# Row-block projections widened to 512 columns, and the order of work around each norm's transposes changed, in a two-block transformer forward pass

## Chip, cores and metric

One core of one Trainium2 chip. The metric is the device time of one execution in microseconds (us), as the median of repeated executions.

## The reference

256 tokens of width 1024 go through two blocks, all in float32. The first has an "even" layer (differential attention, a gated short convolution, cross attention to a 256-token memory) and an "odd" layer (forgetting attention, cross attention), each behind an RMS norm. The second has HGRN2 with a convolution, then a pooling mixer, each followed by cross attention and a gated feed-forward, with a layer norm behind every one of the six steps:

```python
for l in range(DEPTH):                       # DEPTH = 2
    y = hybrid_ab_mixer(x, ...) if l == 0 else multiscale_pool_mixer(x, ...)
    x = layer_norm(ALPHA * x + y, ln_mix_g[l], ln_mix_b[l])
    y = memory_cross_attention_2(x, mem_n, xa_wq[l], xa_wk[l], xa_wv[l], xa_wo[l])
    x = layer_norm(ALPHA * x + y, ln_xa_g[l], ln_xa_b[l])
    y = swiglu_ffn(x, ffn_wg[l], ffn_wu[l], ffn_wd[l])        # D_FF = 2816
    x = layer_norm(ALPHA * x + y, ln_ffn_g[l], ln_ffn_b[l])
```

## The kernel before

**Weights come in units of 1 MB**, 194 of them, in the order of the list PHASES. A unit is loaded by SyncE (SP) into one of two slots of w_raw; ScalarE (ACT) rounds each half of it to w_hi (`hi`, line 1119) and VectorE (DVE) puts the remainder into w_lo (`lo`, line 1675); TensorE (PE) then forms each float32 product as three fp32r products, hi·hi, hi·lo, lo·hi (`passes`, lines 502 to 504). SP loads unit v once the remainder of unit v-2 is made; ACT rounds a half of unit v once PE is done with that half of unit v-2. All engines run fixed programs and meet at semaphores: lo_done and half_done count two per unit, evacuated counts evictions.

**Three kinds of unit.** A K8 unit (`k8_unit`) is 1024 rows by 256 columns of a matrix and takes 48 products 256 columns wide. With weights_stationary the weights are loaded into the array and the tokens move; the result is transposed. Without it the tokens are loaded, 128 at a time, and the 256 weight columns move: these are the row blocks. Each K8 unit fills one PSUM bank; banks 0 and 1 take turns, so that a bank is evicted by ACT (`step`, `copy_out`, line 1141) while the next unit runs. A DN unit (`down_unit`) is 256 rows by 1024 columns, 24 products 512 wide into four banks that stay open over the phase. A feed-forward unit (`half_unit`, lines 836 and 838) loads weights and moves u_hi and u_lo together (512 wide) and u_hi alone (256 wide): 32 products.

**Turns.** A normed activation must be transposed before the next projection. There are nine turns: mem, x, h1 (RMS), h2 (the plain residual), mem2, mix0, xa0, mix1, xa1. PE transposes (`turn_pairs` line 599, `turn_tile` line 610) four groups into banks 6 and 7, ACT rounds each to u_hi (`turned_hi`, `tile_hi` line 1197), DVE writes u_lo (`turned_lo`, `tile_lo` line 1797) and raises tL. A transpose of group n waits for tL of group n-2. In layer norms the last DN unit signals its first token tile by tile0_out and the second by half_done; DVE adds the residual (`res_tile`, line 1816), takes statistics (`tile_ask`, line 1699; the power is POOL's) and norms (`norm_tile`, lines 1737 and 1740). Two K8 units that don't need the new activation run on PE meanwhile (`kv_beside_turn`, `beside_norm`; xk1a, xk1b, half of xv1, o_kv); h2 and xa1 have none.

**The order around a turn before.** ACT, in the second of those units: `hi` of half 0 of the unit after next, first tile, eviction, second tile, `hi` of half 1. DVE (`norm_beside`, `split_beside`): residual and statistics of tile 0, residual of tile 1, a `lo`, statistics of tile 1, norm of tile 0, a `lo`, norm of tile 1, then tile 0's remainder, `lo`, tile 1's remainder, `lo`. At h2 DVE norms the second block's memory (four operations, lines 1737 and 1740) ahead of the residual.

## Time and profile before

| | |
|---|---|
| median of 3 executions | 1379.06 us (1378.71 to 1382.15) |
| the profiled execution's own time | 1384.16 us |
| its span in the trace | 1382.4 us |
| PE / DVE / ACT busy | 94% / 65% / 49% |
| mean granted clock of PE | 0.97 of full |
| chain that ended last | PE 77%, DVE 12%, ACT 4%, DMA 3%, issue 3% |
| bytes read from HBM | 217.54 MB, 158 GB/s |

Busy time of PE counts from the start of a product to its modelled end, and products overlap in it; how long a product holds the engine is read from one start to the next. In timelines the columns are start, length, engine and line, operation, tiles, shapes, count, and in brackets the idle time before it and what ended it. A granted clock of 1.00 is 2.4 GHz, 0.50 is 1.2 GHz.

### The profile page before, as it was taken

Reading aid. Unit: us, or ns where it says so; the run is one execution under the profiler, and the core shown is the slowest. Engines: PE = TensorE matmul, PEld = TensorE weight load, DVE = VectorE, ACT = ScalarE, POOL = GpSimd, SP = SyncE. Lnnn points to the kernel's source line nnn. Section 1 sums busy time; section 2 is a strip of 40 time slices with the busy share of each in tenths; the row PEclk is TensorE's granted clock in tenths of the full one; section 3 lists DMA queues with packets and bytes.
Section 4 is the critical chain, followed back from the end, with each engine's and each line's share of the span. In section 5 each row is a group of like instructions: output and inputs, shape, how many; then the busy total and the mean of one; then the engine's idle time right before and its main releaser. Section 6 shows DMA issues by size and latency. Waiting matters only on the chain.

```text
span 1382.4 us, 21858 instructions
## 1 busy us (share of the span) xinstructions
PE 1304.6 (94%) x8566; PEld 1189.4 (86%) x8566; DVE 898.5 (65%) x1281; ACT 682.1 (49%) x1082; POOL 63.3 (5%) x72
## 2 busy tenths in 40 slices
PE   6999998999999998989989899899999998899996
PEld 6999997889999997889988798788888896788885
DVE  6566576775756555579977755666667755666666
ACT  5445676454436777347424353444444353444442
POOL 0012001000110000000000000000000100000000
PEclk9999999999989999999999999899999999899998
DMA  7455533254535332644425543665555443455552
GB/s 241 158 186 183 174 124 123 96 180 153 188 119 158 114 123 92 230 144 152 153 92 164 171 153 122 227 201 189 182 182 183 137 169 122 150 185 183 184 187 84
DMA packets 167923, 219.67 MB, mean 159 GB/s; under 512 B 3691, under 2 KB 151478, under 8 KB 167846
## 3 DMA queue, kind: packets, MB, share of 16 engines
q1 hardware_dynamic: 164502, 206.68, 45.6%
q0 software_dynamic: 3040, 11.20, 2.6%
q8 instruction: 53, 0.87, 0.3%
q10 hardware_dynamic: 304, 0.73, 0.1%
q14 instruction: 24, 0.20, 0.0%
HBM read 217.54 MB, written 1.05 MB: 158 GB/s over the span
## 4 chain that ended last, share of the span: by engine, by line
PE 77%; DVE 12%; ACT 4%; DMA 3%; issue 3%; POOL 1%; DVEq 0%; SPq 0%; ACTq 0%
PE bank L502 16%; PE bank L504 16%; PE bank L503 16%; PE bank L836 12%; PE bank L838 6%; DVE w_lo L1675 3%; DVE small L1699 1%; DVE h L1816 1%; ACT w_hi L1119 1%; PE bank L713 1%; PE bank L742 1%; DVE att L1737 1%; PE bank L729 1%; DVE att L2273 1%; DMA w_raw<-in_o_w_out 1%
## 5 line engine op out<-in xcount | busy, mean ns | idle before, releaser
L1675 DVE TENSOR_TENSOR w_lo<-w_raw,w_hi 128x1024 fp32r<-128x1024 f32 x388 | 472.2, 1224 | 303.4 <-ACT w_hi L1119 298.2
L1119 ACT ACTIVATE w_hi<-w_raw 128x1024 fp32r<-128x1024 f32 x388 | 408.9, 1058 | 433.1 <-PE bank L504 247.8
L836 PE MATMUL bank<-u_s,w_hi 128*128 128x512 f32 x704 | 254.5, 405 | 1.1 <-DVE u_s L1797 1.1
L502 PE MATMUL bank<-w_hi,y_hi 128*128 128x512 f32 (+1 forms) x656 | 234.4, 357 | 4.5 <-DVE w_lo L1675 3.5
L503 PE MATMUL bank<-w_lo,y_hi 128*128 128x512 f32 (+1 forms) x656 | 229.5, 350 | 0.0
L504 PE MATMUL bank<-w_hi,y_lo 128*128 128x512 f32 (+1 forms) x656 | 229.5, 350 | 0.0
L838 PE MATMUL bank<-u_s,w_lo 128*128 128x256 f32 x704 | 199.9, 284 | 0.0
L502 PE MATMUL bank<-w_hi,u_s 128*128 128x256 f32 x672 | 193.1, 287 | 2.2 <-DVE w_lo L1675 2.2
L503 PE MATMUL bank<-w_lo,u_s 128*128 128x256 f32 x672 | 191.2, 285 | 0.0
L504 PE MATMUL bank<-w_hi,u_s 128*128 128x256 f32 x672 | 191.2, 284 | 0.0
L836 PEld LDWEIGHTS bank<-u_s,w_hi 128*128 128x128 f32 x704 | 134.9, 192 | 35.5 <-DVE u_s L1797 1.9
L502 PE MATMUL bank<-u_s,w_hi 128*128 128x256 f32 x544 | 157.8, 290 | 2.1 <-DVE u_s L1797 2.1
L503 PE MATMUL bank<-u_s,w_hi 128*128 128x256 f32 x544 | 155.3, 285 | 0.0
L504 PE MATMUL bank<-u_s,w_lo 128*128 128x256 f32 x544 | 155.3, 285 | 0.0
L502 PEld LDWEIGHTS bank<-w_hi,y_hi 128*128 128x128 f32 x656 | 125.5, 191 | 23.1 <-DVE w_lo L1675 2.8
L504 PEld LDWEIGHTS bank<-w_hi,y_lo 128*128 128x128 f32 x656 | 125.3, 191 | 16.6
L503 PEld LDWEIGHTS bank<-w_lo,y_hi 128*128 128x128 f32 x656 | 125.6, 191 | 15.0
L838 PEld LDWEIGHTS bank<-u_s,w_lo 128*128 128x128 f32 x704 | 135.5, 192 | 0.7
L502 PEld LDWEIGHTS bank<-w_hi,u_s 128*128 128x128 f32 x672 | 130.1, 194 | 3.0 <-DVE w_lo L1675 2.6
L503 PEld LDWEIGHTS bank<-w_lo,u_s 128*128 128x128 f32 x672 | 130.1, 194 | 0.0
L504 PEld LDWEIGHTS bank<-w_hi,u_s 128*128 128x128 f32 x672 | 130.0, 194 | 0.0
L502 PEld LDWEIGHTS bank<-u_s,w_hi 128*128 128x128 f32 x544 | 105.9, 195 | 3.2 <-DVE u_s L1797 3.2
(296 smaller groups left out, 1642.4 us busy)
## 6 DMA issues: line engine op xcount, KB each, us to landing
w_raw<-in_e_w_in SPq DMA_DIRECT2D x28, 1024.0 KB, 5.1
w_raw<-in_o_w_in SPq DMA_DIRECT2D x28, 1024.0 KB, 5.2
w_raw<-in_ffn_wg SPq DMA_DIRECT2D x22, 1024.0 KB, 5.3
w_raw<-in_ffn_wu SPq DMA_DIRECT2D x22, 1024.0 KB, 5.4
w_raw<-in_ffn_wd SPq DMA_DIRECT2D x22, 1024.0 KB, 5.0
w_raw<-in_ab_w_in SPq DMA_DIRECT2D x12, 1024.0 KB, 5.1
w_raw<-in_e_w_out SPq DMA_DIRECT2D x8, 1024.0 KB, 4.9
w_raw<-in_o_w_out SPq DMA_DIRECT2D x8, 1024.0 KB, 5.0
```

Of the source, the lines that this page charges most:

```text
L502: pe.matmul(out_ap, ah, bh, start=start, stop=False, skip_group_check=True)
L503: pe.matmul(out_ap, ah, bl, start=False, stop=False, skip_group_check=True)
L504: return pe.matmul(out_ap, al, bh, start=False, stop=stop_, skip_group_check=True)
L713: mm = pe.matmul(bank[SC[pr]][:, SEQ * m:SEQ * m + SEQ], XQT[:, 2 * hd + j, P * m:P * m + P], (KT2 if g < 32 else KT1)[:, 2 * hd + j, :], ...
L729: mm = pe.transpose(bank[PTB][:, dst:dst + P], s[:, src:src + P], ident)
L742: mm = pe.matmul(o[:, SEQ * j:SEQ * j + SEQ], V2[:, k, cs], p[:, SEQ * k:SEQ * k + SEQ], start=(k == 0), stop=(k == 1))
L836: pe.matmul(two(bank[banks[m]][:, :], SEQ), w_hi[:, a:a + P], u_both[:, :, SEQ * k:SEQ * k + SEQ], start=(k == 0), stop=False, skip_group_ ...
L838: mm = pe.matmul(bank[banks[m]][:, 0:SEQ], w_lo[:, a:a + P], uh[:, k, :], start=False, stop=(k == 7), skip_group_check=True)
L1119: act.activation(w_hi[:, at:at + 1024], w_raw[:, at:at + 1024], ACT.Copy).then_inc(hi_done, 1)
L1675: v.tensor_tensor(w_lo[:, at:at + 1024], w_raw[:, at:at + 1024], w_hi[:, at:at + 1024].bitcast(F32), ALU.subtract).then_inc(lo_done, 1)
L1699: mark(v.bn_stats(bn6[:, 12 * m + 6 * j:12 * m + 6 * j + 6], src[:, m, 512 * j:512 * j + 512]))
L1737: mark(v.scalar_tensor_tensor(nrm[:, m], src[:, m], mv[:, m, 0:1], gain, ALU.subtract, ALU.mult))
```

## The change

Row blocks: two adjacent units now hold rows 0 to 511 and rows 512 to 1023 of the same 512 columns (`pairs` on SP). PE makes 24 products 512 wide of each into two banks, one per token tile, that stay open over the pair (`row_unit`). ACT evicts both at the pair's end, bank 0 on row0_done, bank 1 on half_done (`row_step`). 58 units are paired: e_kv 4, e_nat 14, e_beside 4, o_kv 4, o_nat 20 of 28, ab_nat 4, xv0 4, xv1 4. In the odd layer the value units now come two by two, with two gate units between. Keys of that layer are normed as 8 and 4 heads, before 6 and 6.

Turns: transposes use four banks, 6, 7, 2, 3, and wait for tL of group n-4. ACT serves both tiles ahead of `hi` (`turn_step`). DVE takes each bank's residual and statistics when that bank is signalled (bank_out). `split_beside` makes the next unit's `lo` first and both remainders after it. At h2 the memory norm comes behind the turn. In the RMS turns the remainders go ahead of one `lo`. At xa1 the first gate and up units run token tile by token tile (`gate_up_tiles`): tile 0 of both, with tile 1's transpose between, then tile 1 of both.

```diff
+            def row_unit(slot, part, banks, xh, xl, wait_lo, wait_bank, fresh=None, between=None):
+                for half in range(2):
...
+                    pe.wait_ge(lo_done, wait_lo + half)
+                    for m in range(2):
+                        if part == 0 and half == 0 and wait_bank is not None:
+                            pe.wait_ge(evacuated, wait_bank + m)
+                        for j in range(2):
+                            k = 4 * part + 2 * half + j
+                            at = 2048 * slot + 1024 * half + 512 * j
+                            mm = passes(bank[banks[m]][:, :], ((xh[:, k, P * m:P * m + P], xl[:, k, P * m:P * m + P]),
+                                                               (w_hi[:, at:at + 512], w_lo[:, at:at + 512])),
+                                        k == 0, k == 7)
+                        if part == 1 and half == 1 and m == 0:
+                            mm.then_inc(row0_done, 1)
+                    mm.then_inc(half_done, 1)
...
-                        if m == 0:
-                            mm.then_inc(tile0_out, 1)
+                            if m == 0 or n == 0:
+                                mm.then_inc(bank_out, 1)
...
-                    pe.wait_ge(tL, n - 1)
+                    pe.wait_ge(tL, n - 3)
...
-                        mm = pe.transpose(bank[6 + n % 2][:, P * k:P * k + P], src[:, m, c:c + P], ident)
+                        mm = pe.transpose(bank[TURN_BANKS[n % 4]][:, P * k:P * k + P], src[:, m, c:c + P], ident)
...
+                def half_tile(slot, banks, half, tile, signal):
+                    ts = slice(P * tile, P * tile + P)
+                    for m in range(2):
+                        o = two(bank[banks[m]][:, :], SEQ)
+                        for k in range(4 * half, 4 * half + 4):
+                            a = 2048 * slot + SEQ * k + P * m
+                            pe.matmul(o[:, :, ts], w_hi[:, a:a + P], u_both[:, :, SEQ * k + P * tile:SEQ * k + P * tile + P],
+                                      start=(k == 0 and tile == 0), stop=False, skip_group_check=True)
+                            mm = pe.matmul(o[:, 0, ts], w_lo[:, a:a + P], uh[:, k, ts],
+                                           start=False, stop=(k == 7 and tile == 1), skip_group_check=True)
...
+            def turn_step(u, first, evac, second):
+                v = u + 2
+                first()
+                evac()
+                second()
+                for half in range(2):
+                    hi(v % 2, half, 16 * (v // 2 + 1), 2 * u + 1 + half)
...
+            def row_step(u, part, pair, banks, out_, i=None, between=None, after=None):
...
+                hi(v % 2, 0, i_land + 16 * (v // 2 + 1), i_half + (2 * u + 1))
...
+                if part == 1:
+                    act.wait_ge(row0_done, pair + 1 if i is None else i + (pair + 1))
+                    out_(0, banks[0])
+                act.wait_ge(half_done, i_half + (2 * u + 2))
+                if part == 1:
+                    out_(1, banks[1])
...
+                hi(v % 2, 1, i_land + 16 * (v // 2 + 1), i_half + (2 * u + 2))
...
             def norm_beside(out_name, name):
 
                 last = UNIT0[out_name] + COUNT[out_name] - 1
-                res_tile(out_name, 0, ALPHA)
-                tile_ask(hv, name, 0)
-                res_tile(out_name, 1, ALPHA)
+                for m in range(2):
+                    for n in range(2):
+                        res_stats(out_name, m, n, ALPHA)
+                    stats_ask(name, m)
                 lo_of(last + 2, 0)
-                tile_ask(hv, name, 1)
                 layer_norm_tile(name, 0)
                 lo_of(last + 2, 1)
                 layer_norm_tile(name, 1)
 
             def split_beside(first):
 
-                tile_lo(uh, ul, 0)
-                lo_of(first, 0)
-                tile_lo(uh, ul, 1)
-                lo_of(first, 1)
+                for half in range(2):
+                    lo_of(first, half)
+                for m in range(2):
+                    tile_lo(uh, ul, m)
                 for half in range(2):
                     lo_of(first + 1, half)
...
+            turned_lo(uh, ul, GCOL["o_norm_g"], 4)
             lo_of(kv + 3, 0)
-            turned_lo(uh, ul, GCOL["o_norm_g"], 4)
             lo_of(kv + 3, 1)
...
-            v.wait_ge(mem_ln_in, 32)
-            for m in range(2):
-                norm_tile(nrm, "mem2", m, MLG, MLB).then_inc(nrm_ready, 1)
             stream("o_out", 6, 1)
...
             stream("o_out", 7, 1)
+            v.wait_ge(mem_ln_in, 32)
+            for m in range(2):
+                norm_tile(nrm, "mem2", m, MLG, MLB).then_inc(nrm_ready, 1)
             stream("ab_t", 0, 1)
...
+                    up1 = UNIT0["ffn1"] + 1
+                    for n in range(2):
+                        res_stats("xo1", 0, n, ALPHA)
+                    stats_ask("xa1", 0)
+                    res_stats("xo1", 1, 0, ALPHA)
+                    layer_norm_tile("xa1", 0)
+                    res_stats("xo1", 1, 1, ALPHA)
+                    stats_ask("xa1", 1)
+                    tile_lo(uh, ul, 0)
+                    layer_norm_tile("xa1", 1)
+                    lo_of(up1, 0)
+                    tile_lo(uh, ul, 1)
+                    lo_of(up1, 1)
```

## Rows read from the trace of the kernel before

**Rows 1.** The page, its part 1: TensorE's busy time.
```profile
PE 1304.6 (94%) x8566; PEld 1189.4 (86%) x8566; DVE 898.5 (65%) x1281; ACT 682.1 (49%) x1082; POOL 63.3 (5%) x72
```

**Rows 2.** Waits of PE, waiter and releaser: us in total, times, longest.
```profile
PE bank L610 <- DVE u_s L1797: 11.6, 4, 5.2
...
PE bank L610 <- DVE h L1740: 6.5, 1, 6.5
...
PE bank L599 <- DVE u_s L1785: 5.7, 2, 3.7
```

**Rows 3.** Groups by shape, PE: first product of each row-block triple on normed rows.
```profile
L502 PE MATMUL bank<-w_hi,u_s 128*128 128x256 f32 x672 | 193.1, 287 | 2.2 <-DVE w_lo L1675 2.2
```

**Rows 4.** Timeline of PE (start, length): first and last L502, 256 wide, then 512 wide.
```profile
74.07 0.28 PE L502 MATMUL bank<-w_hi,u_s 128*128 128x256 f32 x1
...
80.55 0.28 PE L502 MATMUL bank<-w_hi,u_s 128*128 128x256 f32 x1
...
261.27 0.58 PE L502 MATMUL bank<-w_hi,y_hi 128*128 128x512 f32 x1
...
293.47 0.39 PE L502 MATMUL bank<-w_hi,y_hi 128*128 128x512 f32 x1
```

**Rows 5.** Timeline of PE, two of the 48 products 12 columns wide, 23 apart.
```profile
380.12 0.25 PE L504 MATMUL bank<-cf_hi,u_s 128*128 128x12 f32 x1
...
382.69 0.25 PE L503 MATMUL bank<-cf_lo,u_s 128*128 128x12 f32 x1
```

**Rows 6.** Timeline of DVE, ACT and PE at the turn mix0.
```profile
786.41 1.28 DVE L1740 SCALAR_TENSOR_TENSOR h<-att,pow_out,nat 128x1024 f32<-128x1024 f32 x1
792.04 1.29 DVE L1797 TENSOR_TENSOR u_s<-bank,u_s 128x512 fp32r<-128x512 f32 x2 [4.34 <-ACT u_s L1197]
...
790.47 1.06 ACT L1119 ACTIVATE w_hi<-w_raw 128x1024 fp32r<-128x1024 f32 x1 [6.60 <-DMA w_raw<-in_xa_wq]
...
795.38 0.58 PE L502 MATMUL bank<-u_s,w_hi 128*128 128x256 f32 x1 [0.56 <-DVE u_s L1797]
```

**Rows 7.** The same at the turn xa0.
```profile
868.79 1.28 DVE L1740 SCALAR_TENSOR_TENSOR h<-att,pow_out,nat 128x1024 f32<-128x1024 f32 x1
...
874.07 1.06 ACT L1119 ACTIVATE w_hi<-w_raw 128x1024 fp32r<-128x1024 f32 x1 [7.82 <-DMA w_raw<-in_ffn_wu]
...
878.98 0.80 PE L836 MATMUL bank<-u_s,w_hi 128*128 128x512 f32 x1 [0.56 <-DVE u_s L1797]
```

**Rows 8.** The same at the turn h2 (588.11: last of four of its kind).
```profile
588.11 1.28 DVE L1740 SCALAR_TENSOR_TENSOR att<-att,pow_out,nat 128x1024 f32<-128x1024 f32 x1
...
592.97 1.09 PE L610 MATMUL bank<-cst,h 128*128 128x128 f32 x8 [2.78 <-DVEq L2238]
...
597.78 0.58 PE L502 MATMUL bank<-u_s,w_hi 128*128 128x256 f32 x1 [0.56 <-DVE u_s L1797]
```

**Rows 9.** Timeline of PE: first product behind the turns xa1 and mix1.
```profile
1182.49 0.80 PE L836 MATMUL bank<-u_s,w_hi 128*128 128x512 f32 x1 [0.56 <-DVE u_s L1797]
...
1108.49 0.39 PE L502 MATMUL bank<-u_s,w_hi 128*128 128x256 f32 x1 [1.03 <-DVE u_s L1797]
```

**Rows 10.** Windows: length, PE, PEld, DVE, ACT, POOL busy (count); granted clock; DMA share; GB/s.
```profile
597.80:601.30 3.50, 3.50 (x16) 3.50 (x17) 2.96 (x3) 0.05 (x1) 0.00 (x0) 0.50 0.00 0
795.40:799.30 3.90, 3.90 (x18) 3.90 (x19) 3.81 (x4) 1.00 (x2) 0.00 (x0) 0.50 0.14 43
879.00:884.60 5.60, 5.60 (x17) 4.82 (x18) 4.09 (x4) 1.00 (x2) 0.00 (x0) 0.50 0.89 300
...
893.00:904.10 11.10, 11.10 (x64) 9.61 (x63) 6.70 (x11) 5.67 (x10) 0.00 (x0) 1.00 0.58 196
```

**Rows 11.** Timeline of DVE: the last layer norm begins.
```profile
1374.19 1.28 DVE L1737 SCALAR_TENSOR_TENSOR att<-h,small,nat 128x1024 f32<-128x1024 f32 x1 [0.24 <-DVE pow_in L1730]
```

**Rows 12.** Timeline of ACT: a late weight copy, and the eviction behind it.
```profile
374.11 1.06 ACT L1119 ACTIVATE w_hi<-w_raw 128x1024 fp32r<-128x1024 f32 x1 [3.79 <-DMA w_raw<-in_o_w_in]
375.07 0.58 ACT L1141 ACTIVATE nat<-bank 128x512 f32 x1
```

More of the change, by code:

```diff
@@ L60, with pair_of @@
 COUNT = {name: n for name, _, n in PHASES}
+PAIRS = (("e_kv", 2), ("e_nat", 7), ("e_beside", 2), ("o_kv", 2), ("o_nat", 10), ("ab_nat", 2), ("xv0", 2), ("xv1", 2))
+PAIR0 = {}
+_k = 0
+for _name, _n in PAIRS:
+    PAIR0[_name] = _k
+    _k += _n
+def pair_of(name, j):
+    if name == "o_nat" and j >= 14:
+        return None if j >= 26 or (j - 14) % 4 >= 2 else PAIR0[name] + 7 + (j - 14) // 4
+    if name not in PAIR0 or j >= 2 * dict(PAIRS)[name]:
+        return None
+    return PAIR0[name] + j // 2
 def unit_end(name):
@@ L117, in z_unit @@
     name, before, _, _ = BESIDE["o"]
-    first = {"C": 1, "Y": C_HEADS}[kind]
-    return BANK0[name] + before + first + (2 if kind == "C" else 1) * (hd // 2) + 1
+    z = hd // 2
+    return BANK0[name] + before + (4 * (z // 2) + 2 + z % 2 if kind == "C" else C_HEADS + z) + 1
 G1_ROWS = [("e_mem_norm_g", 8), ("e_norm_g", 8)]
@@ L393, in k8, with pairs, unit @@
                 return base + n
+            def pairs(base, w, c0, n):
+                def unit(base_j, half, i):
+                    rows_of = w[512 * half:512 * half + 512, :]
+                    src = rows_of[:, bass.ds(512 * i + c0, 512)] if i is not None else rows_of[:, c0:c0 + 512]
+                    v = 2 * base_j - 2
+                    load(base_j % 2, base_j < 2, v if i is None else 4 * i + v, src.rearrange("(k p) n -> p k n", p=P))
+                if n < 4:
+                    for half in range(2):
+                        unit(base + half, half, None)
+                else:
+                    with sp.Fori(0, n // 2) as i:
+                        for half in range(2):
+                            unit(base + half, half, i)
+                return base + n
             def dn(base, w, n, order=None):
@@ L519, in k8_unit @@
                         for k in range(4 * half, 4 * half + 4):
-                            at = 2048 * slot + SEQ * k
-                            o = bank[bk][:, SEQ * m:SEQ * m + SEQ]
-                            first = half == 0 and m == 0 and k == 0
-                            end = k == 7
-                            if weights_stationary:
-                                a = at + P * m
-                                mm = passes(o, ((w_hi[:, a:a + P], w_lo[:, a:a + P]), (xh[:, k, :], xl[:, k, :])),
-                                            first, end)
-                            else:
-                                mm = passes(o, ((xh[:, k, P * m:P * m + P], xl[:, k, P * m:P * m + P]),
-                                                (w_hi[:, at:at + SEQ], w_lo[:, at:at + SEQ])), first, end)
@@ L531, in k8_unit @@
-                    mm.then_inc(half_done, 1)
-            def k8_phase(name, xh, xl, weights_stationary, n=None, skip=0, fresh=None):
+                            a = 2048 * slot + SEQ * k + P * m
+                            mm = passes(bank[bk][:, SEQ * m:SEQ * m + SEQ],
+                                        ((w_hi[:, a:a + P], w_lo[:, a:a + P]), (xh[:, k, :], xl[:, k, :])),
+                                        half == 0 and m == 0 and k == 0, k == 7)
+                    mm.then_inc(half_done, 1)
@@ L657, in st_turn_qk @@
                     pe.wait_ge(qk_ready, {"A": 1, "X": 2, "C": 3, "Y": 5}[kind])
-                if kind == "C" and hd == C_HEADS // 2:
+                if kind == "C" and hd == 8:
                     pe.wait_ge(qk_ready, 4)
@@ new lines, in row_stream @@
+            def row_stream(name, skip, n, dst, func=ACT.Copy):
+                base, kb = UNIT0[name] + skip, BANK0[name] + skip
+                if n >= 4:
+                    with act.Fori(0, n // 2) as i:
+                        for j in range(2):
+                            row_step(base + j, j, pair_of(name, skip), (kb % 2, (kb + 1) % 2), row_out(dst, i, func), i)
+                else:
+                    for j in range(n):
+                        row_of(name, skip + j, row_out(dst, 0, func))
@@ L1323, in attention @@
                         continue
+                    if kind == "K8" and pair_of(phase, j) is not None:
+                        row_of(phase, j, row_out(eV, j // 2) if name == "e" else row_out(oV, (j - before) // 4),
+                               between=exponentials)
+                        continue
                     if kind == "DN":
@@ L1570, in _ @@
                 if layer == 1:
-                    stream("xv1", 0, 2, nat_dst(V2))
+                    row_stream("xv1", 0, 2, V2)
                     for c in range(4):
```

322 lines of the change are left out of this document (192 added, 130 removed).

## Prediction

> **What bounds the kernel now.** The page comes first: PE is busy 94% of the span, DVE 65% [rows 1]. The table of waits shows what PE's idle time is: its largest entries are transposes (lines 599 and 610) that wait for DVE around a turn [rows 2]. So the streams between the turns go at PE's pace, and a turn costs what its chain takes. The group of the row blocks gives their number [rows 3]: 672 triples, 42 units of 16; with 16 units on the memory they are the 58 that the change pairs. The pace is read from starts in the timeline [rows 4]: from 74.07 to 80.55 us there are 54 products 256 wide, 0.120 us each; from 261.27 to 293.47 there are 141 products 512 wide, 0.228 us each. Last I read the two queues around each turn [rows 6 to 8] and the granted clock behind them [rows 10].
>
> **Part 1, the width.** A row unit goes from 48 x 0.120 = 5.76 us to 24 x 0.228 = 5.48 us, 0.28 us less. The work on the other engines stays: as many `hi`, `lo`, DMAs and evicted columns. A pair does evict two banks at its end where each unit evicted one; ACT's 0.58 us for bank 0 [rows 12] should lie beside PE's last six products (1.37 us), and bank 1's beside the next pair's first six. Where PE waits for something else the 0.28 us is no gain: e_kv's and o_kv's first units are in part 2, xv0's first 2.5 units wait for the convolution's taps on DVE, one e_kv unit runs at half clock, xv1's four wait for DVE's norm. I count 46 of 58 units: 12.9 us. **Here a rule speaks against the change.** The Trainium skill, page "TensorE: Matmul & The Clock Gate", section "Back-to-back issue gap", has a matmul take its columns over 2.4 GHz plus 2.5 ns; by that, pairing saves 24 x 2.5 ns = 0.06 us per unit and the part is worth an estimated 2.8 us. The rows show 0.120 and 0.228, that is 13 ns and more over the columns, and the sum goes by them.
>
> **Part 2, the RMS turns (x and h1).** The third transpose waits for tL of the first group: 3.7 us at the start, the rest of 5.7 us at h1 [rows 2]. In front of it stood, on ACT, a `hi` that waits for a load (or an eviction and a `hi`), and on DVE one `lo` of 1.2 us. Both now stand behind. At x ACT reaches the tiles one `hi` and 0.8 us of eviction earlier; the load of unit 2 still leads: 1.5 us. At h1 the wait goes whole (2.0 us), and the two o_kv units ahead give 0.3 us each of which half counts before the norm is the later: 3.0 us with what the smaller stages give. What was moved back, the `lo` of unit kv+3, is needed a whole unit (5.5 us) later.
>
> **Part 3, h2.** Four memory norm operations of 1.28 us [rows 8] stand on DVE ahead of the residual and end at 589.39, with a `lo` pair and four residual additions behind them, while PE stops at 592.97 - 2.78 = 590.19. Without them the residuals are done with the DN unit's end. Then: 1.1 us for tile 0's transposes, 0.5 for half of tile 1's, 0.6 ACT, 0.7 DVE, 0.3 for signals: the first product at 593.4 in place of 597.78, 4.4 us. The moved norm is needed only in the middle of the unit after, 8 us later.
>
> **Part 4, mix0 and xa0.** ACT serves tile 0 only behind a `hi` that waits for a load until 790.47 [rows 6], 874.07 at xa0 [rows 7]; DVE had normed tile 1 by 787.69 and 870.07. With the tiles ahead, DVE is the bound: after its norm two `lo` (1.2 each), tile 0's remainder (1.3), the first half of tile 1's (0.7): 787.7 + 4.4 = 792.1 against 795.38, 3.3 us; 870.1 + 4.4 = 874.5 against 878.98, 4.5 us. The two `hi` moved back take 2.1 us and their `lo` 2.4; PE comes to that unit 5.7 us after the start. SP's next load waits for the `lo` of the first unit, which now ends some 5 us earlier, so no load is put off. Statistics by bank don't help here: DVE is already saturated from the DN unit's end.
>
> **Part 5, the clock.** After these three turns the granted clock is 0.50 for 3.5, 3.9 and 5.6 us, in which PE did 16, 18 and 17 products [rows 10]. At full clock 16 and 18 take 1.9 and 2.2 us; in the feed-forward 64 take 11.10 us or a little more (0.1775 each), 17 take 3.0. The losses are 1.6, 1.7 and 2.6 us. With the idle time ahead of each turn's first product down from 4 to 5 us to about 2, I take it that the clock stays up: 5.9 us. The bound below is nothing, if it falls as before.
>
> **Part 6, mix1, xa1, the end.** At mix1 PE waits 1.03 us for the remainders [rows 9], which ACT's order delayed; DVE norms tile 1 by 1102.6 and with the same 4.4 us gives the start at 1107.0: 1.4 us. At the end DVE's last norms begin at 1374.19 [rows 11], led by the signal of a whole tile; the first bank is signalled six products earlier: 1.4 us. At xa1 PE idled 6.5 us [rows 2]. Tile 0's norm now comes before tile 1's last statistics, 2.2 us earlier, and the gate starts on tile 0 alone at about 1177.9, not 1182.49 [rows 9]. But the two units are cut into 128 products, half 256 and half 128 wide. No row shows 128-wide products of this kind in a stream; products 12 wide still start every 2.57 / 23 = 0.112 us [rows 5], and 256-wide ones every 0.120, so one of 128 lies between. I take 0.12: 15.4 us against 64 x 0.1775 = 11.4. With the transposes between (1.0), a wait for a `lo` (0.7) and the clock at half until about 1183 (2.3), the third unit begins near 1197.2; before it began near 1182.49 + 11.4 + 2.6 = 1196.5, with the half clock's loss as at xa0: 0.7 us lost; bounds 3 us either way, since the clock may rise earlier or later.
>
> **The sum.** 12.9 + 1.5 + 3.0 + 4.4 + 3.3 + 4.5 + 5.9 + 1.4 + 1.4 - 0.7 = 37.6 us. The profiled execution took 1384.16 us (span 1382.4), 5.1 over the median: it becomes 1346.6. The median of 1379.06 becomes 1341.5. A difference under 0.3%, about 4 us, could not be told from none.
>
> **Rivals.**
> (a) The clock falls at the turns as before. For it: transposes alone did not keep the clock up at h2, where it fell behind 2.8 us of idle time and two sets of transposes. Against: the turns keep far less idle time. Without the 5.9 us: 1347.4. Chance 0.18.
> (b) 512 columns cost twice 256 in these units (0.240), so that the width gives nothing: 1341.5 + 12.9 = 1354.4. For it: in the feed-forward a 512 and a 256 take 0.355 together, more than 0.228 + 0.120. Against: the DN rows move the very same w_hi and w_lo layout at 0.228. The figures of the Trainium skill in part 1 lead almost there: with 2.8 us for 12.9 the estimate would be 1351.6. Chance 0.06.
> (c) The reordering of the turns brings nothing, since the norm on DVE and not ACT's order holds PE; only the width and the end stay: 1379.1 - 14.3 = 1364.8. Against: the waits on DMA ahead of ACT's `hi` in rows 6 and 7. Chance 0.09.
> (d) Slower. Pairs have no spare bank: the next pair's first product needs bank 0 evicted, and in ACT's queue that eviction stands behind `hi` of half 0, which waits for a load. A load that lands L after PE frees its slot delays PE by L + 1.06 + 0.6 - 2.74 us. Row 374.11 has L = 2.8 [rows 12], PE having freed that half at 371.3; were that so in every second unit of the pairs, 29 x 1.7 = 49 us come on top: 1391. It decides from L = 2.4 on, where 29 x 1.3 = 37.6. Against: the late loads in the row phases fall on first units of pairs, where nothing is evicted. Chance 0.05.
>
> The forecast keeps 0.62. The range takes in (a) and the bounds of the clock and of xa1: 1331 to 1354. Faster by over 0.3%: all but (d) and a remainder of (c), 0.93; the same 0.02; slower 0.05.
>
> **What the profile after would show.** Right, if the 512-wide products of the row blocks start 0.228 us apart; if ACT's tile copies at mix0 and xa0 come ahead of `hi` and PE's wait for line 1797 shrinks from 11.6 us to under 6; if the granted clock is 1.00 after h2, mix0 and xa0. Wrong, if waits of PE for ACT's evictions show in the row phases, if the 128-wide products start more than 0.12 us apart, or if DVE's `lo` becomes what PE waits for in the streams.

## The result, and the profile after

The kernel after takes 1359.45 us (median, 1358.64 to 1361.91); the kernel before, on the same chip, 1380.61 (1378.71 to 1382.94). The ratio is 0.985, 95% interval 0.983 to 0.987: 21 us faster, where the forecast had 37.6, and outside its range of 1331 to 1354. Span against span, 1382.4 and 1356.9, it is 25.5 us; the profiled execution of before was longer than any of its timed runs. The steps below are compared in that frame, in which the forecast's 37.6 us is 12.1 us too much; by the medians it is 16.4 us too much.

The page after, as [rows 1], its granted clock in 40 slices, and its chain:

```profile
PE 1286.8 (95%) x7238; PEld 1112.4 (82%) x7238; DVE 897.7 (66%) x1281; ACT 681.5 (50%) x1074; POOL 62.0 (5%) x72
...
PEclk9999999999999998999989999899999999999998
...
PE 74%; DVE 13%; ACT 5%; DMA 4%; issue 3%; POOL 1%; DVEq 0%; SPq 0%; ACTq 0%
```

The waits of PE after, as [rows 2] (total, times, longest):

```profile
PE bank L832 <- DVE att L2097: 7.1, 4, 3.7
PE bank L899 <- DVE nat L2194: 4.8, 1, 4.8
PE bank L534 <- DVE w_lo L1832: 4.6, 5, 1.6
PE bank L672 <- DVE h L1901: 4.4, 1, 4.4
PE bank L661 <- issue: 3.9, 1, 3.9
PE bank L534 <- DVE u_s L1958: 3.9, 3, 1.8
...
PE bank L534 <- ACT nat L1269: 2.5, 4, 0.8
PE bank L534 <- ACT nat L1245: 2.1, 1, 2.1
...
PE bank L899 <- DVE u_s L1958: 1.8, 1, 1.8
PE bank L925 <- DVE u_s L1958: 1.8, 1, 1.8
...
PE bank L534 <- ACT mkv L1277: 1.3, 2, 0.7
```

Lines 672, 661 and 1958 are the 610, 599 and 1797 of before. The transposes (line 610, now 672) waited 11.6 us for the remainders before and don't wait for them now. The first products behind the turns do, 3.9 + 1.8 + 1.8 = 7.5 us, where before it was 3.2:

```profile
PE bank L502 <- DVE u_s L1797: 2.1, 3, 1.0
...
PE bank L836 <- DVE u_s L1797: 1.1, 2, 0.6
```

So the waits for the remainders went from 14.8 to 7.5 us. The 3.9 us of line 661 are at the turn of x, where PE idled 1.43 and 3.67 us before. Line 832's waits, inside the attention, are 7.1 us as before. The 4.8 us of line 899 are new: one wait, in the first steps of ffn0.

PE, the steady row phase (19 such products from the first to the last, 54 products of all three kinds), as [rows 4]:

```profile
74.35 0.39 PE L534 MATMUL bank<-w_hi,u_s 128*128 128x512 f32 x1
...
86.59 0.39 PE L534 MATMUL bank<-w_hi,u_s 128*128 128x512 f32 x1
```

12.24 / 54 = 0.227 us a product of 512. Then PE's first product behind h2, mix0, xa0 and mix1, and xa1's turn with its first product, as [rows 6 to 9]:

```profile
577.80 0.38 PE L534 MATMUL bank<-u_s,w_hi 128*128 128x256 f32 x1 [1.04 <-DVE u_s L1958]
...
770.52 0.38 PE L534 MATMUL bank<-u_s,w_hi 128*128 128x256 f32 x1 [1.82 <-DVE u_s L1958]
...
848.87 0.50 PE L899 MATMUL bank<-u_s,w_hi 128*128 128x512 f32 x1 [1.81 <-DVE u_s L1958]
...
1083.74 0.39 PE L534 MATMUL bank<-u_s,w_hi 128*128 128x256 f32 x1 [1.02 <-DVE u_s L1958]
...
1149.94 1.41 PE L672 MATMUL bank<-cst,h 128*128 128x128 f32 x8 [4.41 <-DVE h L1901]
1153.13 0.58 PE L925 MATMUL bank<-u_s,w_hi 128*128 128x256 f32 x1 [1.78 <-DVE u_s L1958]
```

A stage that starts earlier than before by more than the stage ahead of it has gained. Start of the same work in both traces, and what was gained up to there:

| start of | before | after | gained so far |
|---|---|---|---|
| attention e | 150.39 | 145.38 | 5.0 |
| o_nat | 309.92 | 300.43 | 9.5 |
| ab_t (behind h2) | 597.78 | 577.80 | 20.0 |
| ab_t behind the memory's turn | 612.59 | 591.08 | 21.5 |
| xk1a | 776.37 | 755.28 | 21.1 |
| mix0's first product | 795.38 | 770.52 | 24.9 |
| xa0's first product | 878.98 | 848.87 | 30.1 |
| ffn0's first down unit | 904.22 | 879.46 | 24.8 |
| xv1's second pair | 1093.85 | 1069.69 | 24.2 |
| mix1's first product | 1108.49 | 1083.74 | 24.8 |
| ffn1's third unit | 1207.86 | 1183.43 | 24.4 |
| end | 1382.4 | 1356.9 | 25.5 |

How sure is such a figure? The trace of experiment 2 below is the kernel before, unchanged up to about 870 us. In it ab_t, its first product behind the memory's turn, xk1a, mix0 and xa0 start at 597.33, 611.90, 774.45, 793.17 and 877.05; by that trace the gains there are 19.5, 20.8, 19.2, 22.7 and 28.2. One stage of one pair of traces is known to 1 or 2 us and no better.

At 848.87 the kernel had 30 us; within 31 us it lost 5 of them again. Four queues in that stretch, after:

```profile
845.05 0.57 POOL L1791 DMA_DIRECT2D nat<-in_ln_ffn_g  x1 [7.18 <-DVE h L1901]
845.61 0.53 POOL L1792 DMA_DIRECT2D nat<-in_ln_ffn_b  x1
846.13 0.53 POOL L1802 DMA_DIRECT2D nat<-in_poolm  x1
846.65 0.92 POOL L1803 DMA_DIRECT2D nat<-in_pool_w  x1
847.56 0.54 POOL L1804 DMA_DIRECT2D nat<-in_pool_scale  x1
...
847.54 0.39 SPq L394 DMA_DIRECT2D w_raw<-in_ffn_wg  x1
...
862.11 1.06 ACT L1214 ACTIVATE w_hi<-w_raw 128x1024 fp32r<-128x1024 f32 x1 [12.42 <-DMA w_raw<-in_ffn_wg]
...
866.72 0.47 PE L899 MATMUL bank<-u_s,w_hi 128*128 128x512 f32 x1 [4.75 <-DVE nat L2194]
```

POOL issues five loads, 3.3 MB, for later stages; SP's load of the second gate tile comes right behind them and lands 14.6 us after its issue, where 5.3 is usual. ACT's `hi` waits 12.4 us for it, DVE's `lo` for `hi`, PE for `lo`. The table of waits names a DVE line of another tile (2194), the last semaphore by time; the chain leads to a DMA. In the kernel before, POOL issued the same five at 870.37 and SP that gate tile at 881.43, 11 us later, and it took 5.4 us.

### The profile page after: what moved, and what is told of

Same layout as the page of the kernel before. It is cut to its first block, busy times and chain, and to the rows that moved or that the text cites. A ratio compares the mean times of both kernels' runs of the same rounds, so it can differ in the third digit from the quotient of the medians.

```text
span 1356.9 us, 19194 instructions
## 1 busy us (share of the span) xinstructions
PE 1286.8 (95%) x7238; PEld 1112.4 (82%) x7238; DVE 897.7 (66%) x1281; ACT 681.5 (50%) x1074; POOL 62.0 (5%) x72
## 3 DMA queue, kind: packets, MB, share of 16 engines
HBM read 217.54 MB, written 1.05 MB: 161 GB/s over the span
## 4 chain that ended last, share of the span: by engine, by line
PE 74%; DVE 13%; ACT 5%; DMA 4%; issue 3%; POOL 1%; DVEq 0%; SPq 0%; ACTq 0%
PE bank L534 16%; PE bank L536 15%; PE bank L535 15%; PE bank L899 11%; PE bank L901 6%; DVE w_lo L1832 4%; ACT w_hi L1214 2%; DVE h L1976 1%; DMA w_raw<-in_ffn_wg 1%; DVE small L1983 1%; PE bank L774 1%; PE bank L803 1%; PE bank L925 1%; PE bank L790 1%; DVE att L2444 1%
## 5 line engine op out<-in xcount | busy, mean ns | idle before, releaser
L534 PE MATMUL bank<-w_hi,y_hi 128*128 128x512 f32 x528 | 211.9, 401 | 5.0 <-DVE w_lo L1832 4.0
L536 PE MATMUL bank<-w_hi,y_lo 128*128 128x512 f32 x528 | 207.1, 392 | 0.0
L535 PE MATMUL bank<-w_lo,y_hi 128*128 128x512 f32 x528 | 207.0, 392 | 0.0
L901 PE MATMUL bank<-u_s,w_lo 128*128 128x256 f32 x672 | 190.1, 283 | 0.0
L899 PEld LDWEIGHTS bank<-u_s,w_hi 128*128 128x128 f32 x672 | 127.7, 190 | 38.8 <-DVE w_lo L1832 5.0
L534 PE MATMUL bank<-w_hi,u_s 128*128 128x512 f32 x336 | 134.9, 402 | 7.1 <-ACT nat L1245 2.1
L536 PE MATMUL bank<-w_hi,u_s 128*128 128x512 f32 x336 | 132.4, 394 | 0.0
L535 PE MATMUL bank<-w_lo,u_s 128*128 128x512 f32 x336 | 132.3, 394 | 0.0
L901 PEld LDWEIGHTS bank<-u_s,w_lo 128*128 128x128 f32 x672 | 128.3, 191 | 0.7
L534 PEld LDWEIGHTS bank<-w_hi,y_hi 128*128 128x128 f32 x528 | 100.0, 189 | 29.4 <-DVE w_lo L1832 4.4
L535 PEld LDWEIGHTS bank<-w_lo,y_hi 128*128 128x128 f32 x528 | 100.0, 189 | 19.6
L534 PEld LDWEIGHTS bank<-u_s,w_hi 128*128 128x128 f32 x544 | 104.9, 193 | 6.0 <-DVE u_s L1958 4.6
L535 PEld LDWEIGHTS bank<-u_s,w_hi 128*128 128x128 f32 x544 | 105.1, 193 | 0.1
L536 PEld LDWEIGHTS bank<-u_s,w_lo 128*128 128x128 f32 x544 | 104.9, 193 | 0.0
L534 PEld LDWEIGHTS bank<-w_hi,u_s 128*128 128x128 f32 x336 | 64.1, 191 | 23.1 <-issue 4.7
```

The source lines that it names most:

```text
L534: pe.matmul(out_ap, ah, bh, start=start, stop=False, skip_group_check=True)
L535: pe.matmul(out_ap, ah, bl, start=False, stop=False, skip_group_check=True)
L536: return pe.matmul(out_ap, al, bh, start=False, stop=stop_, skip_group_check=True)
L899: pe.matmul(two(bank[banks[m]][:, :], SEQ), w_hi[:, a:a + P], u_both[:, :, SEQ * k:SEQ * k + SEQ], start=(k == 0), stop=False, skip_group_ ...
L901: mm = pe.matmul(bank[banks[m]][:, 0:SEQ], w_lo[:, a:a + P], uh[:, k, :], start=False, stop=(k == 7), skip_group_check=True)
```

## The experiments

**1 and 2. Is it the collision, and did the change make it?** POOL's loads of this stage are held back, in the kernel after and in the kernel before.

```diff
+                if i == 2:
+                    pool.wait_ge(half_done, 2 * (UNIT0["ffn0"] + 6))
                 pool.dma_start(LNG, g.to_broadcast([P, D])).then_inc(ln_in, 16)
+                if i == 2:
+                    pool.wait_ge(half_done, 2 * (UNIT0["ffn0"] + 8))
                 pool.dma_start(LNB, b.to_broadcast([P, D])).then_inc(ln_in, 16)
...
+                    pool.wait_ge(half_done, 2 * (UNIT0["ffn0"] + 10))
                     pool.dma_start(PM.rearrange("p g n -> p (g n)"), t["poolm"]).then_inc(pool_in, 16)
...
```

(and units 12 and 15 for the last two). In the kernel after:

> The kernel after, with GpSimd's five loads of the ffn0 stage (3.3 MB: the layer norm's two rows and the three pooling tables, issued at 845.05 to 847.56) held back behind units 6, 8, 10, 12 and 15 of the feed-forward, one at a time. Theory (collision): the load of the second gate tile, issued at 847.54, takes 14.6 us only because it shares the DMA engines with them; alone it should land in 5 to 6 us, ScalarE's 12.4 us of idle time and TensorE's 4.8 us wait at 861.97 go, and the half clock behind that wait too: the first 25 us of the feed-forward last about 25 us as before the change, not 30.6. Time lower than the kernel after by 5 to 8 us, 1352 to 1354. Rival (the tables cost their time wherever they are): the stall moves into the middle of ffn0, whose 134 us from 896 to 1031 grow by 4 us or more, and the total stays at 1358 to 1360.

Measured: 1351.0 us (1350.25 to 1355.29), ratio to before 0.979 (0.977 to 0.980). The same `hi`, now waiting for PE and no longer for its load, and the stretch 849 to 862 in windows (length, PE, PEld, DVE, ACT, POOL busy with counts, granted clock, DMA share, GB/s):

```profile
852.54 1.06 ACT L1214 ACTIVATE w_hi<-w_raw 128x1024 fp32r<-128x1024 f32 x1 [3.73 <-PE bank L901]
...
849.00:862.00 13.00, 13.00 (x67) 11.29 (x67) 6.15 (x7) 6.36 (x10) 0.00 (x0) 0.87 0.61 203
```

and the same window of the kernel after:

```profile
849.00:862.00 13.00, 12.97 (x64) 10.90 (x64) 2.68 (x3) 0.69 (x1) 0.00 (x0) 0.87 1.04 358
```

The DMA engines were full (358 GB/s, share 1.04) and are not now (203); ACT and DVE, busy for 0.69 and 2.68 us of it in the kernel after, now make the next weights for 6.36 and 6.15. The new wait is gone; from xa0's first product to the first down unit it takes 848.00 to 871.89, 23.9 us, against 30.6 after and 25.2 before. The loads, spread over ffn0, cost nothing there (190.1 us from that unit to xv1's second pair, 190.2 after). By the medians the run is 8.4 us faster than the kernel after, a little more than expected; of the 7.7 us between the spans, 6.7 lie in this stretch, and 0.9 it was ahead by already at h2, where nothing was changed. In the kernel before:

> The kernel before, with the same five loads held back in the same way. Theory (collision made by the change): before, they were issued at 870.37 and the second gate tile at 881.43, so that it landed in 5.4 us; nothing to win, time within 1.5 us of the kernel before. Rival (the tables always cost several us at this place, and the change is not to blame): it is faster by 4 us or more.

Measured: 1381.19 against 1381.66, ratio 1.000 (0.999 to 1.001). The same loads are harmless there. The collision came with the change.

**3. Who brought the loads together?** ACT's and DVE's order at mix0 and xa0 is put back.

```diff
-                turn_step(u + 1, lambda: tile_hi(uh, 0), evac, lambda: tile_hi(uh, 1))
+                    step(UNIT0[name] + j, copy_out(dst, j), BANK0[name] + j,
+                         between=(lambda: tile_hi(uh, 0)) if last else None,
+                         after=(lambda: tile_hi(uh, 1)) if last else None, b=unit_bank(name, j))
...
+                    tile_lo(uh, ul, 0)
+                    lo_of(first, 0)
+                    tile_lo(uh, ul, 1)
+                    lo_of(first, 1)
```

In the kernel after:

> The kernel after with the order around the turns of mix0 and xa0 put back: ScalarE makes the next weights' high halves ahead of the turned tiles again, and VectorE the low halves in between. The single signals of the banks stay. By the trace of after the two layer norms give back 3.75 and 5.0 us. Theory (the new order is also what brought the loads together: the low halves of the next weights are made earlier, so the second gate tile's buffer comes free at 847.5, right behind GpSimd's loads): the 6.6 us of the collision are won back, so the kernel is only 1 to 4 us slower than after, 1360 to 1363. Rival (the collision came from the stages having moved together, whatever the order): it stays, and the kernel is 8 to 10 us slower, 1367 to 1369.

Measured: 1360.71 us (1358.86 to 1366.53), a difference of 1.3 us to the kernel after. Its queues:

```profile
850.21 0.57 POOL L1789 DMA_DIRECT2D nat<-in_ln_ffn_g  x1 [7.18 <-DVE h L1899]
...
859.57 0.39 SPq L394 DMA_DIRECT2D w_raw<-in_ffn_wg  x1
...
871.02 0.47 PE L899 MATMUL bank<-u_s,w_hi 128*128 128x512 f32 x1 [0.34 <-DVE nat L2198]
```

The gate tile's load is 9 us behind POOL's again and PE waits 0.34 us, not 4.75. In its trace mix0 starts 3.5 us and xa0 another 3.8 us later than in the kernel after, and then 5.6 us come back. So in the kernel as changed the new order at these two norms is worth almost nothing. Without the collision to hide its price:

> The same order put back, in the kernel with GpSimd's loads held back, where no collision hides its price. Theory: slower than that kernel (1351.0) by the 3.75 and 5.0 us of the two layer norms, less what of it the single signals carry: 6 to 9 us, 1357 to 1360. Rival (the prediction's rival c: VectorE ends its chain no sooner, whatever the order): under 2 us slower.

Measured: 1360.15 us, 9.1 more than 1351.0; in the traces 3.5 at mix0, 3.8 at xa0, 0.3 behind it, and 1.1 at xa1, where nothing was changed and the clock was at half for 10.1 us instead of 6.7 (below). The order is worth 7.3 us at the two norms where the forecast said 7.8, and rival (c) falls.

**4. The width.** Each product of 512 is made as two of 256 in the same bank, all else as in the kernel after.

```diff
-                            mm = passes(bank[banks[m]][:, :], ((xh[:, k, P * m:P * m + P], xl[:, k, P * m:P * m + P]),
-                                                               (w_hi[:, at:at + 512], w_lo[:, at:at + 512])),
-                                        k == 0, k == 7)
+                            for c in (0, SEQ):
+                                mm = passes(bank[banks[m]][:, c:c + SEQ],
+                                            ((xh[:, k, P * m:P * m + P], xl[:, k, P * m:P * m + P]),
+                                             (w_hi[:, at + c:at + c + SEQ], w_lo[:, at + c:at + c + SEQ])),
+                                            k == 0 and c == 0, k == 7)
```

> The kernel after, each product of 512 columns in the row pairs made as two of 256 in the same bank, with the same weights, waits and evictions. 26 pairs (52 units of 96 instead of 48 products). Theory: a product of 256 costs 0.120 us against 0.228 for 512, 0.28 us a unit: where TensorE is the bound, 14.6 us for 52 units, so slower than after by 9 to 14 us (the units beside the attention, where TensorE waits for others, give less or nothing). Rival 1 (width buys nothing, the gain of the first 150 us came from the order of the turns and the spare banks): slower by under 4 us. Rival 2 (a longer unit costs no more than its waits give back, as the attention showed): slower by 5 to 8 us.

The pairs are 29 and not 26: the page counts 8630 products against 7238, which is 58 x 24 more.

```profile
PE 1302.7 (95%) x8630; PEld 1190.7 (87%) x8630; DVE 898.2 (65%) x1281; ACT 682.4 (50%) x1074; POOL 62.0 (5%) x72
```

Measured: 1371.31 us (1368.22 to 1373.71), 11.9 more than the kernel after and 12.9 more than experiment 5, which ran beside it. The width is worth about the forecast's 12.9 us for part 1, though by all 58 units and not by 46, and with executions from 1368.22 to 1373.71 us this is known to some 3 us. Rival (b) falls. Where it paid: its trace, one of its slower executions, 14.8 us behind that of after in the end, is behind by 5.4 us at 145, 8.0 at 300, 13.4 at 399 and 15.0 at 479 us; from ab_nat to mix0's turn, eight units, nothing comes on top (14.4 at 578, 13.4 at 640, 13.8 at 764). What becomes of the gain in that stretch, the next one asks.

**5. ab_nat's banks.** The first pair opens two banks at once, one of them just being evicted; here it takes banks 6 and 7.

```diff
+            if name == "ab_nat" and j < 2:
+                return 6 + j
...
-                         kb - 1 if kb else None, fresh, between)
+                         kb - 1 if kb and (name != "ab_nat" or first) else None, fresh, between)
```

> The kernel after, with the first pair of ab_nat in banks 6 and 7 (free since the turns of mem2) in place of 0 and 1, so that it waits for no eviction. Theory: the 1.8 us that were lost between 597.8 and 647.2 of before are the pair's need of two banks at once, the second of them just being emptied; TensorE's waits of 1.51 us at 627.53 and 2.08 us at 631.24 shrink to the 1.5 us for the weights that the kernel before had there. Time lower than after by 1.5 to 2.5 us. Rival: ScalarE's queue (the gate's exponentials and logarithms ahead of the weight halves) is what is late, TensorE then waits for w_lo for as long, and the time stays within 0.7 us.

Measured: 1358.41 us (1357.1 to 1359.66), 1.0 less. After:

```profile
631.24 0.50 PE L534 MATMUL bank<-w_hi,u_s 128*128 128x512 f32 x1 [2.08 <-ACT nat L1245]
...
704.70 1.97 PE L1100 MATMUL bank<-cst,nat 128*128 128x128 f32 x8 [3.75 <-DVEq L1826]
721.74 1.99 PE L1108 MATMUL bank<-att,ones 128*128 128x256 f32 x8 [2.13 <-DVEq L1826]
```

and with the spare banks:

```profile
634.78 0.50 PE L536 MATMUL bank<-w_hi,u_s 128*128 128x512 f32 x1 [1.72 <-DVE w_lo L1834]
...
703.40 1.97 PE L1102 MATMUL bank<-cst,nat 128*128 128x128 f32 x8 [3.75 <-DVEq L1828]
719.82 3.17 PE L1110 MATMUL bank<-att,ones 128*128 128x256 f32 x8 [2.47 <-DVEq L1828]
```

The wait for the eviction is gone and PE is 2.1 us ahead at 640; at the convolution's mean (line 1108 after, 1110 here) it still is by 1.9, and at 729 by 0.2. DVE's operation that the mean waits for, and the clock behind it, after and with the spare banks:

```profile
720.34 1.29 DVE L2542 TENSOR_TENSOR att<-att,bank 128x512 f32<-128x512 f32 x2
...
720.50:723.90 3.40, 2.17 (x10) 1.92 (x11) 2.48 (x4) 0.26 (x1) 0.00 (x0) 1.00 0.73 280
```

```profile
718.43 1.28 DVE L2544 TENSOR_TENSOR att<-att,bank 128x512 f32<-128x512 f32 x2
...
720.50:723.90 3.40, 3.40 (x10) 2.68 (x9) 1.42 (x3) 0.00 (x0) 0.00 (x0) 0.50 0.99 365
```

DVE came 1.9 us earlier too, so here it was not DVE that kept the gain back: 3.4 us at half clock behind the mean took 1.7 of the 1.9 us. That DVE can hold PE at this place, a later run shows (the last but one of experiment 8). Why the clock fell here and not in the kernel after is open.

**6. xa1 by tiles.** The first gate and up units of ffn1 are made over both tiles again, with experiment 1's loads.

```diff
-                    turn_normed("xa1", 0)
+                    for m in range(2):
+                        turn_normed("xa1", m)
...
-                    gate_up_tiles(2 * base + 1, kb, hs, (end - 2, end), lambda: turn_normed("xa1", 1))
+                gate_up(0, 2 * base + 1, kb, hs if hs else None, (end - 1, end))
```

> The kernel with GpSimd's loads held back, and the first gate and up tiles of ffn1 made from whole 256 columns again, behind both turned tiles. Theory (as the sum had it, minus 0.7 us for xa1): 96 extra products at 0.115 us cost about what the earlier start gives, so the time stays within 1.5 us of 1351.0. Rival (starting on the first tile saves the idle time, as the change intends): slower by 3 us or more.

Measured: 1353.32 us (1350.12 to 1356.19) against 1351.0 (1350.25 to 1355.29); the ratios' intervals, 0.9785 to 0.9817 and 0.9772 to 0.9802, overlap, and the profiled span is 0.9 us shorter; from mix1's first product to ffn1's third unit it takes 99.5 us against 99.7, although without the tiles the clock is at half for 13.5 us in it and with them for 6.7. The tiles bring too little to be told from nothing.

**7. The single signals.** A residual waits for its whole tile again.

```diff
-                if m == 1 and n == 1:
+                if m == 1:
                     v.wait_ge(half_done, unit_end(name))
                 else:
-                    v.wait_ge(bank_out, 3 * outputs.index(name) + 2 * m + n + 1)
+                    v.wait_ge(bank_out, 3 * outputs.index(name) + 2)
```

> The kernel with GpSimd's loads held back, and the residual sums waiting for a whole tile (both banks) as before the change; the order around the turns and the sums' halves with their statistics stay. A bank's last products are 6 of 512 columns, 1.4 us, so that VectorE starts 1.4 us later at five layer norms and at the end of the kernel. Theory (each tile's chain is bound by VectorE's start): slower by 1 to 1.4 us at each of mix0, xa0, mix1, xa1 and the last, 5 to 7 us in all, 1356 to 1358. Rival (the second tile's chain sets the end, and its first bank comes late anyway): 0 to 2.5 us.

Measured: 1359.23 us, but from 1352.82 to 1364.52, and the profiled execution, the lowest, has a span only 1.8 us longer than that of experiment 1. It was 1.8 us ahead at xk1a, and lost 3.6 from there: 0.4 at mix0, 0.8 up to xa1, 1.1 at xa1, 1.3 at the end. The median says 8, the trace 3.6. What differs between executions had to be found first: the next experiment.

**8. The clock.** Extra products, which nobody reads, fill idle time of PE: 9 behind the last turn of mix0 and of xa0, 28 ahead of xa1's first turn.

```diff
+            def keep_busy(b, n):
+                for i in range(n):
+                    pe.matmul(bank[b][:, 0:SEQ], yh_[:, 8, 0:P], yh_[:, 9, :], start=True, stop=True,
+                              skip_group_check=True)
...
                 turn_normed(name, 1)
+                keep_busy({"mix0": 4, "xa0": 0}[name], 9)
...
+                    keep_busy(4, 28)
                     turn_normed("xa1", 0)
```

> The kernel with GpSimd's loads held back, and extra products whose results nobody reads, in TensorE's idle time: 9 of 256 columns (1.08 us at 0.120) behind the last turns of mix0 and of xa0, where it idles 1.82 us, and 28 (3.4 us) in the 4.4 us wait ahead of the turns of xa1. Nothing else is changed, and no work is moved. Theory (the half clock of about 3.3 us that follows each of these idle times comes from them, so that with gaps under 1.1 us the granted clock stays at 1.00): 1.6 us won at mix0, 1.6 at xa0 and 2.5 to 3 at xa1, 5 to 6 us in all, 1345 to 1346 against 1351.0. Rival 1 (the fall has another cause, what the engine did long before or the chip's state): the clock falls as before and the time stays within 1 us. Rival 2 (the extra products end late and put the turns or the first products back): slower by 1 us or more.

Measured: 1348.46 us (1346.67 to 1350.06), ratio 0.975 (0.973 to 0.977), the lowest median here; the interval just touches experiment 1's. Windows behind mix0's, xa0's and xa1's first product, without the extra products (experiment 1):

```profile
769.70:773.20 3.50, 3.50 (x20) 3.50 (x21) 2.76 (x3) 0.75 (x1) 0.00 (x0) 0.66 0.99 318
848.10:851.60 3.50, 3.50 (x15) 2.96 (x15) 2.71 (x3) 0.71 (x1) 0.00 (x0) 0.67 0.89 293
1145.50:1149.00 3.50, 3.50 (x17) 3.50 (x17) 3.46 (x3) 0.00 (x0) 0.78 (x2) 0.50 0.01 2
```

and with them:

```profile
770.80:774.30 3.50, 3.50 (x29) 3.50 (x30) 2.78 (x3) 0.79 (x1) 0.00 (x0) 1.00 1.01 294
847.60:851.10 3.50, 3.50 (x20) 3.04 (x21) 2.79 (x3) 0.79 (x1) 0.00 (x0) 1.00 0.92 295
1143.90:1147.40 3.50, 3.50 (x17) 3.50 (x18) 3.46 (x3) 0.00 (x0) 0.78 (x2) 0.53 0.01 2
```

At mix0 and xa0 the clock stays at 1.00, and the stretches behind them shrink: from mix0's first product to xa0's it takes 76.8 us, not 78.35, and from there to ffn0's first down unit 22.7, not 23.9. At xa1 two idle times of 1.05 and 2.10 us are left, and the clock still falls. Theory right at two places of three; 2.5 us won of the 5 to 6 expected. More of it, with ab_nat's banks and at two further places:

> All of it together: GpSimd's loads held back, the first pair of ab_nat in banks 6 and 7, and the extra products in the idle times of mix0, xa0 and xa1. Theory: the spare banks give under 1 us by themselves, since TensorE then waits for VectorE's convolution (the trace of that run: 2.1 us earlier at 639.8, 0.2 at 729.1), so 0 to 1 us below the run before it. Rival: with the clock staying up, their gains add, 1.5 us or more below it.

Measured: 1349.0 us, ratio 0.975 (0.973 to 0.977): no gain. The time is the theory's, but in the trace the lead at the gated output again goes in a half clock at the mean (0.50 from 723.4 to 726.8, where experiment 8's first run has 1.00).

> The fastest kernel so far with more of the idle time filled: 26 products (3.1 us) ahead of the turn of the gated output, where TensorE idles 3.74 us and runs 4.6 us at half clock behind it, and 9 (1.08 us) between the turns of xa1's first tile and its first product, where it idles 2.10 us and then runs 3.3 us at half clock. Theory: at xa1 1.3 to 1.7 us are won; at the gated output the products come 2 us earlier, but TensorE then waits for VectorE's convolution, as with the spare banks, so 0 to 0.7 us there: 1346.5 to 1347.5. Rival (both gains add): 1344.5 to 1345.5.

(26 products by `keep_busy(6, 26)` ahead of the wait for hg_y, 9 by `keep_busy(4, 9)` behind `turn_normed("xa1", 0)`.) Measured: 1348.76 us (1347.15 to 1351.55), not told apart from 1348.46. PE at the gated output and the convolution's mean:

```profile
704.50 1.09 PE L1108 MATMUL bank<-cst,nat 128*128 128x128 f32 x8 [0.64 <-DVEq L1843]
720.92 3.43 PE L1116 MATMUL bank<-att,ones 128*128 128x256 f32 x8 [4.10 <-DVEq L1843]
```

Line 1100's idle time of after is filled and its clock kept. By 710 us PE has gained 2.5 us on the first run of this experiment, and 2 of them stand as idle time ahead of the mean: 4.10 against 2.13. Here DVE holds PE. The rest and more goes in the half clock behind that idle time (0.50 from 720.5 to 723.8). At xa1 the trace shows 1.4 us won, and 1.7 lost ahead of mix1, where the clock fell behind an idle time of 1.93 us; behind 1.83 us at the same place it had stayed in the first run.

With the gaps filled, the single signals once more, the edit of experiment 7 on experiment 8:

> The fastest kernel so far (GpSimd's loads held back, extra products in the idle times; 1348.5 us) with the residual sums waiting for a whole tile again. The same edit without the extra products gave 1359.2 as a median of runs from 1352.8 to 1364.5, but only 1.8 us more in the trace of its lowest run. Theory (what the late signals cost by themselves is the 0.4 to 0.5 us of longer idle time at each turn; the rest was the clock falling or not behind those gaps): with the gaps filled it is 2 to 3.5 us slower, 1350.5 to 1352. Rival (the single signals are worth more in themselves): slower by 5 us or more.

Measured: 1353.21 us (1351.89 to 1354.97), 4.75 more than 1348.46. The spread fell from 11.7 to 3.1 us, but the price lies between theory and rival. In the trace the stages from h2 on lose 0.4 at mix0, 0.5 at xa0, 0.4 at xa1 and 1.3 at the end, 2.6 us by the signals; another 3.4 us by half clock, behind idle times of 1.92 us at the pooling's mixing and of 1.47 us at xa1, 0.1 and 0.4 us longer than without this edit. They are worth 2.6 us and what the clock makes of it.

## Why the prediction was wrong, point by point

The direction and most terms were right. Three steps failed. The forecast took it that no load is put off (6.7 us), that the clock stays up behind the turns (2.85 us), and that ab_nat's and xv0's units pay in full, with no new wait and no half clock there (1.9 us). The first is shown by experiments 1 to 3; the sizes of the other two come from one pair of traces.

- **Part 1 (12.9).** Right where PE sets the pace. From o_nat's start to o_out's the gain goes from 9.5 to 15.6 us (543.40 before, 527.84 after): 6.1 us, where 20 units at 0.28 are 5.6. Halving all the widths costs 11.9 to 12.9 (experiment 4). The rule set against it (the Trainium skill, "TensorE: Matmul & The Clock Gate", "Back-to-back issue gap") would have given an estimated 2.8. The section gives that gap for a single product, apart from a stream with weight loads, and 512 columns at 0.227 beside twice 0.120 do not follow it. What failed is the rest: from 591 to 755 us the gain sank from 21.5 to 21.1 where 5.5 units should have added 1.5, 1.9 us short (by experiment 2's trace 3.2). In this stretch PE's idle times over 1 us are 1.55, 4.71 and 2.35 us before and 1.51, 2.08, 3.75 and 2.13 after, 0.9 us more, with the eviction's 2.08 at 631.24 as the new one; and it worked for 8.8 us at half clock, before for 6.6, which is 1.1 us more. The forecast put this wait at nothing, since "the late loads in the row phases fall on first units of pairs, where nothing is evicted": the first pair behind units of one bank opens two, and one was just being evicted. Without the eviction (experiment 5) the gain was lost to the clock instead, so what it would be worth by itself stays open.
- **Parts 2 and 3 (4.5, 4.4).** At h2 the gain goes from 15.6 at o_out's start to 20.0: 4.4. Part 2 has no reading of its own: 15.6 less 11.3 (40.5 units at 0.28) leaves 4.3. The wait of 2.04 us at h1 is gone, and at x PE idles 3.9 us where it was 5.1; but at x it also ran 5.1 us at half clock before and 3.3 after, so some of the 4.3 is the clock's.
- **Part 4 (7.8).** 3.75 and 5.0 at the two first products, 1 us more than said; experiment 3 gives 7.3 for the order alone. But the step "SP's next load waits for the `lo` of the first unit, which now ends some 5 us earlier, so no load is put off" is the one that failed worst. It followed SP's queue and not POOL's: the earlier load fell onto 3.3 MB of POOL's. Experiments 1 to 3: 6.7 us lost.
- **Part 5 (5.9).** The step "I take it that the clock stays up" failed for two of three. Behind h2, 1.04 us idle, it did: 1.5 of 1.6 us. Behind mix0 and xa0, 1.8 us idle, it fell: 0.2 of 1.7, and by experiment 1 1.35 of 2.6. Even the 1.35 are in part chance: the stretch from xa0's first product to the first down unit takes 25.2 us in the trace of before, 23.7 in experiment 2's and 23.9 in experiment 1's. Rival (a) was this, at 0.18. 2.85 us short.
- **Part 6 (2.1).** mix1 0.6 of 1.4, the end 1.1 of 1.4, xa1 -0.4 where -0.7 was forecast: 0.8 short. The 128-wide products: a pair of 256 and 128 starts every 0.231 us, so 0.111 beside 0.120; the 0.12 taken was close.
- Another 0.6 us went between ffn0's start and xv1's second pair. By experiment 2's trace of before there is no such loss (21.3 us gained at the one, 21.5 at the other), so it is within what two traces differ by.

The sum: 37.6 - 1.9 - 0.2 + 0.95 - 6.7 - 2.85 - 0.8 - 0.6 = 25.5 us, the difference of the spans. It closes because it is read from one pair of traces; with experiment 2's span the gain is 22.5, and by the medians 21. Of the 12.1 missing, 6.7 are the collision, and experiment 1 wins them back. Rival (d), late evictions, is there as a mechanism (2.1 us once, 0.8 and less elsewhere), 5.9 us in all for its 49. Its waits for evictions were one of the signs named for "wrong", and they came, small. Of the three signs named for "right", the products are 0.227 us apart, as said. The tile copies come first; of the wait for line 1797 the 11.6 us at the transposes are gone, but all waits for that line are 7.5 us and not under 6. The clock is at 1.00 behind h2 alone. The prediction also calls the transposes of lines 599 and 610 the largest waits of the table; the second largest, 7.1 us, is the attention's line 771, and the change left it as it was.

## What to carry to other kernels

When a step's reordering lets a buffer come free sooner, look at every DMA queue for what is issued in the microseconds around the new time, not only at the queue that loads the buffer; a bulk load that nobody needs for 200 us belongs where the loads have slack. Count a gain as time only up to the next date that another engine sets: of 2.5 us that PE won ahead of the convolution's mean by full clock, 2 came back as idle time there. And idle times near 2 us are worth closing, since a half clock of 3.4 us, 1.7 us lost, may stand behind each.

## What the runs showed of the hardware

- Behind idle times near 2 us the granted clock is not the same from one trace to the next of nearly the same program. Where it fell, it was at 0.50 for 3.4 us or more (771.7 to 775.1 behind mix0 and 850.2 to 853.6 behind xa0 in the kernel after). Behind 1.81 us at xa0 it fell in the kernel after and in experiments 1, 4 and 6, and stayed at 1.00 in experiment 5. Ahead of the pooling's mixing (line 1180) it fell behind 1.93 and 1.92 us in the last two runs of experiment 8, and stayed behind 1.92 us in the kernel after, 1.97 in experiment 5 and 2.23 in the second run of experiment 8. Behind 1.04 us at h2 it stayed in every run, behind 3.6 to 3.75 us at the gated output it fell in every run that left this idle time open. What decides between the two near 2 us, no run here shows. Filling an idle time with products that nobody reads (experiment 8) kept it up at mix0 and xa0 in four traces, and at the gated output in the one that filled it.
- So a median hides two things, the edit's own price and how many of these idle times it moves across that edge. One trace, stage by stage, tells the first: 3.6 us where the median said 8, of which 2.6 were the edit's own by the last run.
- Loads on two queues slowed each other: 3.3 MB on one made the 1 MB of the other take 14.6 us, not 5.3, at 358 GB/s together. Spread over ffn0 one at a time, they cost no wait.
